# Six block openings of a two-layer streaming encoder: the statistic of x by one matmul with a block of ones, and the last four steps tile by tile

## The reference

```python
def _rms_norm(x, g):
    y = xf * lax.rsqrt(jnp.mean(xf * xf, axis=-1, keepdims=True) + EPS)
    return y * g
def _layer(x, ...):
    x = x + 0.5 * _rms_norm(_swiglu(_rms_norm(x, ffn1_pre), up, down), ffn1_post)
    m = _mixer(_rms_norm(x, mix_pre), ...)      # GLA, differential attention, retention; W_in 1024 x 3344
    x = x + _rms_norm(m, mix_post)
    x = x + 0.5 * _rms_norm(_swiglu(_rms_norm(x, ffn2_pre), up, down), ffn2_post)   # 1024 -> 2 x 2816 -> 1024
```

## Time and profile before

| | |
|---|---|
| median of 3 runs | 1379.61 us (1379.55 to 1383.23) |
| the profiled execution | 1380.57 us, its span 1378.8 us |
| TensorE matmuls | 1348.1 us, 98% of the span, x9709 |
| VectorE, ScalarE, GpSimd | 804.5 us (58%), 634.1 us (46%), 131.2 us (10%) |
| granted TensorE clock, mean | 0.992 |
| DMA | 187.51 MB, mean 136 GB/s |

### The profile page before, as it was taken

How to read it: one execution, slowest core, us unless ns; L and a number is a source line. 1 busy time by engine, 2 the same in 40 slices (tenths; PEclk the granted TensorE clock), 3 DMA queues, 4 the chain that set the end, 5 groups by cost and what they waited for, 6 DMA issues and landing times.

```text
span 1378.8 us, 24882 instructions
## 1 busy us (share of the span) xinstructions
PE 1348.1 (98%) x9709; PEld 1309.5 (95%) x9709; DVE 804.5 (58%) x1230; ACT 634.1 (46%) x1001; POOL 131.2 (10%) x131
## 2 busy tenths in 40 slices
PE   6999999999999999999999999999899999999998
PEld 6999999988889999999999999999789899999998
DVE  5655544677666665554466555446776676555542
ACT  4544433553356544434454444445434665444433
POOL 2000000351000300000030000003600020000000
PEclk9999999999999999999999999999999999999999
DMA  5655555453344455545545554455333345555452
GB/s 151 192 170 169 160 165 152 114 153 82 94 119 119 110 150 152 152 142 143 158 109 151 152 149 143 144 160 143 90 83 93 100 123 145 146 151 152 140 152 67
DMA packets 351754, 187.51 MB, mean 136 GB/s; under 512 B 6320, under 2 KB 348604, under 8 KB 351688
## 3 DMA queue, kind: packets, MB, share of 16 engines
q1 hardware_dynamic: 348368, 177.49, 45.8%
q0 software_dynamic: 2480, 8.10, 1.7%
q10 hardware_dynamic: 840, 0.99, 0.3%
HBM read 182.24 MB, written 4.33 MB: 135 GB/s over the span
## 4 chain that ended last, share of the span: by engine, by line
PE 88%; issue 4%; POOL 3%; DVE 2%; ACT 1%; DMA 1%; DVEq 1%; ACTq 0%; POOLq 0%; SPq 0%
PE ps L633 27%; PE ps L634 26%; PE ps L635 26%; POOL x L520 1%; PE ps L696 1%; PE ps L831 1%; PE ps L932 1%; PE ps L806 1%; PE ps L689 1%; DVE w_l L512 1%; PE ps L945 0%; DVE z L1531 0%; DMA par_in<-in_ret_norm_dram 0%; PE ps L904 0%; DVE probs L1472 0%
## 5 line engine op out<-in xcount | busy, mean ns | idle before, releaser
L633 PE MATMUL ps<-xn_l,w_h 128*128 128x320 f32 x1840 | 579.3, 315 | 2.4 <-DVE xn_l L1306 2.4
L634 PE MATMUL ps<-xn_h,w_l 128*128 128x320 f32 x1840 | 567.9, 309 | 0.0
L635 PE MATMUL ps<-xn_h,w_h 128*128 128x320 f32 x1840 | 567.8, 309 | 0.0
L512 DVE TENSOR_TENSOR w_l<-raw,w_h 128x1024 fp32r<-128x1024 f32 (+1 forms) x340 | 408.1, 1202 | 179.9 <-ACT w_h L503 179.8
L503 ACT ACTIVATE w_h<-raw 128x1024 fp32r<-128x1024 f32 (+1 forms) x342 | 353.1, 1035 | 243.9 <-DMA raw<-in_ffn_w_down_dram 129.3
L633 PEld LDWEIGHTS ps<-xn_l,w_h 128*128 128x128 f32 x1840 | 345.7, 188 | 11.8 <-issue 5.0
L634 PEld LDWEIGHTS ps<-xn_h,w_l 128*128 128x128 f32 x1840 | 346.0, 188 | 1.0
L635 PEld LDWEIGHTS ps<-xn_h,w_h 128*128 128x128 f32 x1840 | 345.7, 188 | 0.0
L633 PE MATMUL ps<-hid_l,w_h 128*128 128x320 f32 x704 | 216.6, 308 | 0.0
L634 PE MATMUL ps<-hid_h,w_l 128*128 128x320 f32 x704 | 216.6, 308 | 0.0
L635 PE MATMUL ps<-hid_h,w_h 128*128 128x320 f32 x704 | 216.6, 308 | 0.0
(11 more groups left out here) (242 smaller groups left out, 1155.0 us busy)
## 6 DMA issues: line engine op xcount, KB each, us to landing
raw<-in_ffn_w_up_dram SPq DMA_DIRECT2D x176, 512.0 KB, 3.9
raw<-in_ffn_w_down_dram SPq DMA_DIRECT2D x64, 448.0 KB, 3.8
raw<-in_w_in_dram SPq DMA_DIRECT2D x54, 512.0 KB, 3.8
raw<-in_ffn_w_down_dram SPq DMA_DIRECT2D x32, 512.0 KB, 4.1
raw<-in_w_out_dram SPq DMA_DIRECT2D x16, 512.0 KB, 4.0
const<-in_tables_dram POOLq DMA_DIRECT2D x8, 298.0 KB, 4.4
x_in<-in_x_prompt_dram SPq DMA_DIRECT2D x1, 1024.0 KB, 6.5
scores<-in_cache_diff_k_dram POOLq DMA_DIRECT2D x2, 512.0 KB, 5.5
```

Source lines behind the costliest of these rows:

```text
L512: dve.tensor_tensor(w_l[s][:, 0:cols], raw[s][:, 0:cols], w_h[s][:, 0:cols], ALU.subtract).then_inc(w_lo, 1)
L633: pe.matmul(out, w_h[s][:, w], xl, start=first, stop=False)
L634: pe.matmul(out, w_l[s][:, w], xh, start=False, stop=False)
L635: return pe.matmul(out, w_h[s][:, w], xh, start=False, stop=last)
```

## The change

The statistic of x and the order at the end of an opening are made otherwise; the statistic of y keeps its way (its semaphores are only counted anew, 3 a layer and not 6).

- VectorE adds ssum_x to ssum as well, once both are there, ahead of the low parts of tiles 4 and 5.
- TensorE makes one float32 matmul with a 128x128 block of ones and the 320 columns of ssum: the sum over the partitions stands in all 128 partitions of PSUM at once. It comes after three of the four tiles are finished.
- ScalarE takes the root of 128x320 values, VectorE the reciprocal of 128x320 values straight into rs. `spread` and the copy are gone from the opening.
- Steps 0 to 3 of the opening go over the four tiles as before; then tile 0 takes its steps 4 to 7, then tile 1, tile 2, the statistic, tile 3.
- In the first two openings the work for lambda comes behind the reciprocal.

```diff
@@ tensor
-            def opening(l, u0, n, norm, m):
-                for i in range(KD):
+            def opening(l, u0, n, m):
+                for i in range(KD // 2):
                     opening_step(l, u0, n, i)
-                    if i == KD - 2:
-                        stat_x(l, norm, m)
-                spread(l, norm)
-
-            def stat_x(l, n, m):
-                pe.wait_ge(x_sum_lo, l * 3 + m + 1)
-                for i in range(3):
-                    pe.matmul(ps_stat[:, i:i + 1], ssum[:, TOK[i]:TOK[i] + P], C("ones")[:, 0:1], start=i == 0, stop=False,
-                              skip_group_check=True)
-                pe.wait_ge(x_sum_hi, l * 3 + m + 1)
-                for i in range(3):
-                    mm = pe.matmul(ps_stat[:, i:i + 1], ssum_x[:, TOK[i]:TOK[i] + P], C("ones")[:, 0:1], start=False, stop=True,
-                                   skip_group_check=True)
-                mm.then_inc(ss_mm, 1)
+                for t in range(OPENING):
+                    if t == OPENING - 1:
+                        stat_x(l, m)
+                    for i in range(KD // 2, KD):
+                        if t == 0:
+                            pe.wait_ge(xn_lo, (l * 4 + n) * KD + i + 1)
+                        tile_part(slot(l, u0 + t), t, i, i + 1)
+
+            def stat_x(l, m):
+                pe.wait_ge(x_sum, l * 3 + m + 1)
+                pe.matmul(ps_stat[:, 0:T], C("ones").broadcast_to([P, P]), ssum[:, :], start=True, stop=True).then_inc(x_stat, 1)
@@ scalar
+            def root_x(l, m):
+                act.wait_ge(x_stat, l * 3 + m + 1)
+                act.activation(sq[0][:, :], ps_stat[:, 0:T], ACT.Sqrt, scale=1.0 / D).then_inc(x_root, 1)
...
                 act.preload_act_table(ACT.Sqrt)
-                root(l, norm)
+                root_x(l, m)
@@ vector
-                dve.tensor_tensor(ssum[:, :], ssum[:, :], y[:, 3, :], ALU.add).then_inc(x_sum_lo, 1)
-
-            def spread_in(l, norm):
-                root(l, norm)
-                dve.tensor_copy(rs[:, :], ps_rs[:, 0:T])
+                dve.tensor_tensor(ssum[:, :], ssum[:, :], y[:, 3, :], ALU.add)
+                dve.drain()
+                dve.wait_ge(x_sum_hi, l * 3 + m + 1)
+                dve.tensor_tensor(ssum[:, :], ssum[:, :], ssum_x[:, :], ALU.add).then_inc(x_sum, 1)
+
+            def root_x(l, m):
+                dve.wait_ge(x_root, l * 3 + m + 1)
+                dve.reciprocal(rs[:, :], sq[0][:, :])
                 dve.drain()
 
             def begin(l, n, norm, m, u0, update):
...
                 for v in (4, 5):
                     lo(dve, l, u0 + v)
+                root_x(l, m)
                 if l == 0 and n == 0:
                     lambda_sums()
                 if l == 0 and n == 1:
                     lambda_final()
-                spread_in(l, norm)
```

More of the change, by code:

```diff
@@ L391, in build @@
         sq_x = sem("sq_x")
-        x_sum_lo, x_sum_hi = sem("sum_of_first_squares"), sem("sum_of_last_squares")
+        x_sum_hi, x_sum = sem("sum_of_last_squares"), sem("sum_of_squares_of_x")
+        x_stat, x_root = sem("mean_square_of_x_replicated"), sem("root_of_mean_square_of_x")
         x_add = sem("x_add")
@@ L683, in stat_y, with spread @@
                 mm.then_inc(ss_mm, 1)
-            def spread(l, n):
-                pe.wait_ge(inv_out, l * 6 + n + 1)
+            def spread(l, m):
+                pe.wait_ge(inv_out, l * 3 + m + 1)
                 for i in range(3):
@@ L705, in up_pair @@
                         tile_part(slot(l, u0 + 2 * q + g), 2 * q + g, 0, KD)
-                opening(l, u0, n, norm, m)
+                opening(l, u0, n, m)
                 up_pair(0, 2, False)
@@ L729, in ffn @@
                 down_pair(KD // 2 - 1)
-                stat_y(l, norm + 1, norm // 2)
+                stat_y(l, norm // 2)
                 if last:
@@ L737, in ffn @@
                 else:
-                    spread(l, norm + 1)
+                    spread(l, norm // 2)
                     keep_busy(6)
@@ L971, in _ @@
                 ffn(l, U_F1, G_F1, 0, 0, 0)
-                opening(l, U_MIX, 1, 2, 1)
+                opening(l, U_MIX, 1, 1)
                 pe.wait_ge(tables_loaded, PIECES * 16)
@@ L989, in _ @@
                     tile_part(slot(l, U_OUT + v), v % 6, 0, KD, HEAD_ORDER, xw_h, xw_l)
-                stat_y(l, 3, 1)
-                spread(l, 3)
+                stat_y(l, 1)
+                spread(l, 1)
                 keep_busy(6)
@@ L1024, in split_hi, with root_y @@
                 act.activation(dst[:, k, :], src[:, k, :], ACT.Copy, scale=scale).then_inc(xn_hi, 1)
-            def root(l, n, half=False):
-                act.wait_ge(ss_mm, l * 6 + n + 1)
+            def root_x(l, m):
+                act.wait_ge(x_stat, l * 3 + m + 1)
+                act.activation(sq[0][:, :], ps_stat[:, 0:T], ACT.Sqrt, scale=1.0 / D).then_inc(x_root, 1)
+            def root_y(l, m, half):
+                act.wait_ge(ss_mm, l * 3 + m + 1)
                 act.activation(var[:, 0:3], ps_stat[:, 0:3], ACT.Sqrt, scale=(4.0 if half else 1.0) / D).then_inc(ss_sqrt, 1)
@@ L1111, in ffn @@
                 y_tile(l, m + 1, None, phase, 3, 1, norm + 1, SLOTS + l * UNITS + d0 + 3 * m + 6)
-                root(l, norm + 1, half=True)
+                root_y(l, phase, True)
             def mixer_step(l, kind, n):
@@ L1234, in _ @@
                         hi(act, l, U_F2 + 3)
-                root(l, 3)
+                root_y(l, 1, False)
                 act.wait_ge(kv_stored, (l + 1) * 64)
@@ L1238, in _ @@
                 ffn(l, U_F2, 4, 3)
-            act.wait_ge(inv_out, DEPTH * 6)
+            act.wait_ge(inv_out, DEPTH * 3)
             for hf in range(2):
@@ L1308, in split_lo, with root_y @@
                 i.then_inc(xn_lo, 1)
-            def root(l, n):
-                dve.wait_ge(ss_sqrt, l * 6 + n + 1)
+            def root_y(l, m):
+                dve.wait_ge(ss_sqrt, l * 3 + m + 1)
                 dve.reciprocal(inv[:, 0:3], var[:, 0:3]).then_inc(inv_out, 1)
-                dve.wait_ge(rs_mm, l * 6 + n + 1)
+                dve.wait_ge(rs_mm, l * 3 + m + 1)
             def add_first(k):
@@ L1420, in ffn, with rows_out @@
                 if l == DEPTH - 1 and f == 1:
-                    rows_out(l, norm + 1)
+                    rows_out(l, phase)
                 else:
-                    root(l, norm + 1)
+                    root_y(l, phase)
                     dve.wait_ge(evac, l * GROUPS + g0 + KF + KD)
-            def rows_out(l, n):
-                dve.wait_ge(ss_sqrt, l * 6 + n + 1)
+            def rows_out(l, m):
+                dve.wait_ge(ss_sqrt, l * 3 + m + 1)
                 dve.reciprocal(inv[:, 0:3], var[:, 0:3]).then_inc(inv_out, 1)
@@ L1634, in _ @@
                         lo(dve, l, U_F2 + 3)
-                root(l, 3)
+                root_y(l, 1)
                 dve.wait_ge(evac, l * GROUPS + G_OUT + N_OUT)
```

2 lines of the change are left out of this document (1 added, 1 removed).

## The result

The changed kernel took 1366.27 us in the median of 6 runs (1364.96 to 1366.84), the kernel before 1379.58 us beside it (6 runs, 1378.68 to 1383.23). The ratio is 0.9904, 95% interval 0.9891 to 0.9916: 13.3 us less. The forecast was 1369.2 us.

What follows compares the result with a forecast made beforehand. TensorE, 98% busy, was taken as the bound. Openings -8.8 and mixers' level 0 wait -1.6 sum to -10.4 us: span 1368.4, profiled execution 1370.2, median 1369.2 us; own range 1366 to 1372, 8 in 10 1363 to 1376.

Steps and rivals of the forecast that it cites:

- What leaves and what comes on TensorE: Each opening: statistic 1.34 and spread 0.67 us leave, new matmul 0.54 comes; 1.47 us won, 8.8 for six.
- The order tile by tile: Openings: low parts of x fall due earlier, but earlier steps hide it with 0.9 us margin; no wait counted.
- rival (d): Opening, tile 0, steps 5 to 7: TensorE waits for x, 1.95 us an opening; 1382.5 us, chance 0.04.
- The factor rs: Openings: 2.15 us reciprocal, rs 3.4 to 3.5 us after the statistic, about 1 us earlier; cost nothing.
- The earlier loads in the mixers: Mixers: loads come earlier, abs 4.8 us earlier, the wait at level 0 goes; 0.8 us each, 1.6 in all.
- In the FFN blocks the earlier loads win nothing, because TensorE waited for no weight there.: FFN blocks: no gain counted from the earlier loads, as TensorE had no wait for weights there.
- it moves with TensorE, and I leave them: Mixers: waits of 0.95 us at the rotation and 2.25 us ahead of level 5 stay, their chain starting from TensorE.
- The shared port, taken as zero: Mixer rotations: VectorE and GpSimd blocking shifts by -1.2 to +0.6 us a rotation, four rotations in two layers; zero taken.
- Rival (c): Hand-overs: lower clock, 1.2 GHz, falls into product matmuls instead; +7.6 us, 1376.8 us, chance 0.09.

Runs made afterwards that it cites:

- e_low: Changed kernel with twelve one-column and six 128-column matmuls, results unread, added back in each opening; 1380.26 us.
- e_order: Kernel before with only the opening's new step order, keeping the old statistic and spread; 1375.38 us, ratio 0.998 to the kernel before.
- e_stat: Changed kernel with the old order of the opening's steps, keeping the new statistic; 1374.73 us, ratio 0.9969 to the kernel before.
- e_late: Changed kernel with the loads into the first three slots behind an opening held until the fourth tile is done; 1383.51 us.
- e_rot: Changed kernel with the fourth rotation of retention moved from behind level 3 to behind level 5; 1370.34 us.
- e_recip2: Changed kernel with the opening's reciprocal, and its drain, made twice in a row; 1369.47 us.
- e_lead: Changed kernel with one high part moved behind logit and one low part behind decay in the mixers; 1365.10 us.
- e_keep4: Changed kernel with four instead of six bridging matmuls at each of the five hand-overs; 1365.93 us.
- e_both: Changed kernel with four instead of six bridging matmuls and e_lead's edit together; 1365.30 us.
- e_near: Changed kernel with GpSimd's first memset of the mixer moved ahead of its first difference; 1365.87 us.

## Why the prediction held, and where it did not

The direction, the place and nearly the size were right: 10.4 us were worked out, and the stretches that repeat show 10.3, or 9.6 with the new wait for the sum of y, which the prediction did not have. At equal clock it is 10.6 (below).

*What leaves and what comes on TensorE.* -1.47 us an opening, 8.8 in all: 222.01 against 220.54 in the FFNs, and e_low gives the 2.01 us of the old work back. The value taken for the new matmul (0.54) was the measured one; the statistic's and the spread's distances were right to 0.01 us.

*The order tile by tile.* No wait for x inside tile 0; rival (d) did not occur.

*The factor rs.* A reciprocal's time does not go by partitions: 2.15 us for 128 as for 44. It is covered, by the 4.45 - 3.36 us that rs comes earlier; the tightest place has 0.3 us.

*The earlier loads in the mixers.* -0.87 us a mixer where 0.8 was forecast, and e_order has it by itself. In the chain behind it abs was put 1.1 us too early, because the fourth load was given 3.9 us and took 5.0. It cost nothing because VectorE was the later of the two in the forecast: its low part 9, worked out for +13.1, is done at +12.6, and ScalarE's factor, worked out from the early abs, is there at +12.7. So the running sum could start at once, with no room left.

*The step that failed* is the sentence "In the FFN blocks the earlier loads win nothing, because TensorE waited for no weight there." It is true of the order alone (222.01 in e_order) and false of the change: with the statistic's 1.47 us gone and the loads as they were, the four FFNs lose 3.0 us of their 5.9 (e_stat). The prediction never asked when a weight's low part is due in an FFN once TensorE comes earlier. Its sum stood only because both were in the diff, and that was luck. In the same way the forecast "it moves with TensorE, and I leave them" held for level 5 (2.24 us), not for the rotation.

*The shared port, taken as zero.* The rotation's wait fell from 0.95 to 0.4 us, and a new one of 0.74 came at level 4: 0.1 to 0.2 us worse a mixer, inside the bounds of -1.2 to +0.6 us. By the rule quoted there (the Trainium skill, SBUF — State Buffer, section on the two separate sides) a blocking could be struck out or added. Here one was eased and one added, and the rows at level 4 agree with it: the late one is held, whichever engine it is, and ends 1.08 us (VectorE) or 1.43 us (GpSimd) behind the other where it takes 1.21 or 1.55 alone. What was missing in the forecast is that such a chain has few states: a shift of 1.1 to 1.3 us (+9.2 to +8.06 and +7.89) took it from one to the next, and which one is read off the starts.

*What was not forecast: the clock.* The median is 2.9 us below the forecast, with the mechanism at its size. Rival (c) had the sign wrong: the low stretches did not move into product matmuls, there were fewer. (Its sum has a slip, too: 5 x 2 - 3 x 0.9 is 7.3 and not 7.6 us, 1376.5.) Before (columns: window, its length, TensorE's busy time, granted clock, DMA share, GB/s):

```profile
20.00:22.30 2.30, 2.30 (x9) 0.50 0.01 3
690.00:695.00 5.00, 4.62 (x16) 0.66 0.31 92
992.00:998.00 6.00, 5.88 (x60) 0.50 0.31 81
```

After, the same kinds of place:

```profile
17.00:22.30 5.30, 3.90 (x23) 1.00 0.61 148
443.00:449.00 6.00, 5.26 (x31) 1.00 0.31 90
990.00:996.00 6.00, 6.00 (x79) 1.00 0.35 92
1113.00:1115.00 2.00, 1.74 (x7) 0.50 0.55 166
1115.00:1119.00 4.00, 4.00 (x19) 0.84 0.00 0
```

0.50 is 1.2 GHz of 2.4. Each execution on record comes with its mean granted clock, to 0.001, and with it the clock's part can be told from the rest. The kernel before has 0.9937 in the mean of 72 executions (0.990 to 0.996), the changed one 0.997 in ten (0.996 to 0.998). Where both had 0.996 (12 and 4 executions) they took 1377.42 and 1366.82 us in the mean: 10.6 us apart. That is the change at equal clock, good to some 0.6 us because the clock is given in steps that are worth about 1 us; the other 2.7 us of the 13.3 go with the higher clock. The halves fit as well: at 0.996 e_order took 1374.48 us (3 executions) and e_stat 1374.33 (4), 2.9 and 3.1 us below before, where their stretches give 2.8 and, with the wait for the sum of y, 3.1. Over ten executions each the clock is 0.9944 in e_order, 0.9956 in e_stat and 0.993 in e_low: the order alone hardly raises it, the statistic alone a little, both raise it more, and the added records take it down again.

Counting in each kernel how far its hand-overs lie above 18.20 us and its stretches from level 5 above 130.33, before has 6.4 and 6.4 us, e_low 6.7, e_order 3.1, e_stat 6.0, e_late 5.2, e_rot 10.2; after 1.8 and 4.5, e_recip2 3.7, e_lead 1.9, e_keep4 2.0, e_both 0.8, e_near 3.0. These figures hold the wait for the sum of y as well (0.7 of the 1.8 in after). One kernel differs from itself by 2.7 us, so a single profile tells little here, and what in the change raises the clock stays open.

## What to carry to other kernels

When TensorE is 98% busy and two of its small operations are cut, price the cut by the distance between starts, not by durations; here it came out to 0.01 us. Then ask of every wait that is zero now how much of it is cover: a gain of 1.5 us a block is lost again in good part where the weights' low parts come just in time, and the edit that seems to win nothing (earlier loads) can be what lets it through. Cost a pair of edits together and each without the other. And before a rest of 2 or 3 us is put down to an edit, compare executions that were granted the same clock.

## What the runs showed of the hardware

- A reciprocal of 320 columns takes 2.15 us on 128 partitions as on 44, 4.4 times an add of the same shape (0.49 us). A root of 128x320 from PSUM on ScalarE takes 0.44 us.
- Where a product of GpSimd and a VectorE instruction with two inputs in SBUF meet here, the later one is held until about the end of the other; in e_low VectorE was first by 0.03 us. The groups of 26 mixers differ by 1.25 us on TensorE's path with it. GpSimd's chain started at +7.5, +7.7 to +8.1 or +9.2 us against level 0, at nothing between.
- The granted clock falls to 0.50 for some us at places that differ between executions of one kernel, also inside a mixer's product work (992 to 998 us, where TensorE had 5.88 us busy of 6.00). In before, executions at a mean of 0.992 took 1381.45 us and at 0.996 1377.42 (9 and 12 of them): 1 us for 0.001, as much as many an edit.
- Loads let go close together land later. Behind the first mixer's opening: 3.8 to 7.3 and 3.8 to 8.3 us (before, e_late) against 3.7 to 5.0 with the first three 1.8 us apart.
- Four bridging matmuls in place of six made no hand-over worse in two executions, and the medians (1365.93, 1365.30) are not above that of after.
